# A transformer step on one core: when a lookup table is copied, and where 48 of 128 expert places run

## The reference

```
def peer_ffn(h, w_q, sub_k1, sub_k2, expert_u, expert_v):
...
    idx = jnp.take_along_axis(cidx, pos, axis=-1)
    gate = jax.nn.softmax(best, axis=-1).astype(h.dtype)
...
        u = jnp.take(expert_u, ib, axis=0)
        act = jax.nn.gelu(jnp.einsum('td,tkd->tk', hb, u))
        vrows = jnp.take(expert_v, ib, axis=0)
        return jnp.einsum('tk,tkd->td', gb * act, vrows)
```

## Time and profile before

| | us |
|---|---|
| median of 3 runs | 4420.11 (4410.85 to 4426.94) |
| the profiled execution's own time | 4409.17 |
| its span in the trace | 4407.6 |

### The profile page before, as it was taken

The page is one execution under the profiler, slowest core; times in us unless marked ns, Lnnn a source line. Parts: engine busy times, 40 slices in busy tenths (PEclk is TensorE's granted clock), DMA queues, the critical chain, the costliest instruction groups (busy, mean ns, idle before and its releaser), DMA issues.

```text
span 4407.6 us, 32479 instructions
## 1 busy us (share of the span) xinstructions
PE 3313.6 (75%) x8957; PEld 1651.8 (37%) x8957; DVE 2481.5 (56%) x4999; ACT 1047.2 (24%) x2847; POOL 1860.9 (42%) x1668
## 2 busy tenths in 40 slices
PE   8666289899926767634987887887887887777776
PEld 5443156556624434312433332333332332222222
DVE  0122055987338777744575675675675675675544
ACT  2101011011112211110333333333333332332322
POOL 0032025776125455510445445445445445445554
PEclk9876599999957877767999999999999999999999
DMA  5698987999388888851999999999999999999998
GB/s 217 218 334 315 320 270 303 395 386 369 140 345 329 298 314 336 295 195 73 370 414 421 420 418 421 404 417 421 407 418 422 404 419 422 418 411 421 422 419 356
DMA packets 301854, 1552.96 MB, mean 352 GB/s; under 512 B 31217, under 2 KB 58865, under 8 KB 179185
## 3 DMA queue, kind: packets, MB, share of 16 engines
q0 software_dynamic: 239616, 1342.28, 77.0%
q1 hardware_dynamic: 47488, 187.83, 11.0%
q10 hardware_dynamic: 14592, 21.10, 1.3%
HBM read 1507.98 MB, written 178.52 MB: 383 GB/s over the span
## 4 chain that ended last, share of the span: by engine, by line
DMA 25%; PE 16%; issue 6%; DVE 3%; ACT 1%; POOL 1%; ACTq 0%; POOLq 0%; DVEq 0%
DMA ring<-uv_d,IXD_p 25%; PE ps L1460 14%; PE ps L1430 3%; DVE ring L1661 2%; POOL ring L1778 1%; ACT dg L1510 1%; ACT GE_p L1504 0%; DVE BV_p L926 0%; DVE ACC L1642 0%; DVE DOT_p L1661 0%; DVE BP_p L931 0%; ACTq L1509 0%; PE ps L1445 0%; PE ps L1423 0%; POOLq L1774 0%
## 5 line engine op out<-in xcount | busy, mean ns | idle before, releaser
L1460 PE MATMUL ps<-ring,dg 128*128 128x512 f32 x3584 | 1699.7, 611 | 455.2 <-ACT dg L1510 432.7
L1778 POOL DMA_INDIRECT ring<-uv_d,IXD_p x896 | 1120.2, 1250 | 1308.3 <-PE ps L1460 1011.4
L1661 DVE CUSTOM_DVE_ANT_0 ring<-ring,H 128x1024 f32<-128x1024 f32 x896 | 1094.6, 1224 | 878.2 <-DMA ring<-uv_d,IXD_p 862.8
L1460 PEld LDWEIGHTS ps<-ring,dg 128*128 128x128 f32 x3584 | 651.5, 192 | 1381.7 <-ACT dg L1510 711.0
L1137 PE MATMUL ps<-w,xg 128*128 128x368 f32 x1792 | 563.6, 476 | 22.4 <-issue 20.2
L1504 ACT ACTIVATE GE_p<-DOT_p 128x2 f32<-128x2 f32 x448 | 91.1, 203 | 1473.3 <-DVE DOT_p L1661 1473.3
L1137 PEld LDWEIGHTS ps<-w,xg 128*128 128x128 f32 x1792 | 342.7, 191 | 242.9 <-issue 30.8
L1510 ACT ACTIVATE dg<-gdi,GE_p 128x128 f32<-128x128 f32 x896 | 310.7, 394 | 55.0 <-PE ps L1460 7.2
L1498 ACT ACTIVATE gdi<-ident,GD_p 128x128 f32<-128x128 f32 x896 | 303.3, 386 | 14.8 <-issue 14.6
L225 POOL DMA_DIRECT2D uv_d<-in_peer_u x128 | 69.4, 543 | 495.1 <-issue 253.9
L1260 POOL DMA_INDIRECT rv<-in_peer_v,IXD x128 | 156.9, 1226 | 260.2 <-DVE AC L1242 229.9
(11 more groups left out here) (364 smaller groups left out, 2718.0 us busy)
## 6 DMA issues: line engine op xcount, KB each, us to landing
uv_d<-in_peer_u POOLq DMA_DIRECT2D x128, 512.0 KB
uv_d<-in_peer_v POOLq DMA_DIRECT2D x128, 512.0 KB
w<-in_w_in SPq DMA_DIRECT2D x8, 2944.0 KB
w<-in_w_in SPq DMA_DIRECT2D x16, 1472.0 KB
z_d<-zo ACTq DMA_DIRECT2D x16, 1288.0 KB
ring<-uv_d,IXD_p POOLq DMA_INDIRECT x896
gates_p<-z_d SPq DMA_DIRECT2D x7, 1536.0 KB
wq_s<-in_peer_w_q SPq DMA_DIRECT2D x8, 1024.0 KB, 13.2
```

The lines of the kernel that those rows point to most:

```text
L1460: mm = T.matmul(bank(6 + n), dg[:, k % DR, :], ring[:, k % RS, D + n * 512:D + (n + 1) * 512], start=(k == 0), stop=(k == NK - 1))
L1661: V.tensor_tensor_reduce(out=row, in0=row, in1=H2[:], scale=1.0, scalar=0.0, op0=ALU.mult, op1=ALU.add, accum_out=DOT[:, k:k + 1]).then_in ...
L1778: g.indirect_dma_start(ring[:, n % RS, :], None, uv_d, bass.IndirectOffsetOnAxis(ap=IXD[:, n:n + 1], axis=0)).then_inc(s_ring[n % RS], 16)
```

## The change

The table's copy leaves the sample stage, the stage of block 1 and the start of the projection stage (`TABLE_BS`, `TABLE_E` and `TABLE_S` are 0). Parts 0 to 15 are issued at the end of the projection stage, behind all its gathers; parts 16 to 127 in the mixer stage, four after each point. POOL now issues a part only when the part two before it has landed.

The first 48 places of block 1 run in the projection stage, behind the places of block 0, through the same ring (`dve_experts_ahead`); their sum goes through `ac_d` in DRAM to the mixer stage. The mixer stage has 80 places of block 1 left, four points in a block instead of six or seven. Point 0, which stood between the transposes and the scores, now stands behind the softmax next to point 1; after it come one point between the merge and the copy of `oaT`, and one before the residual. Of the values three groups are left behind the last block instead of seven. ACT's places move: `GATES_AT` 12 to 4, gelu of group g to `n` = 9 + 10g, and two more gelus at `n` = 92 and 100 and a third after 111.

```
-TABLE_BS, TABLE_E, TABLE_CS = 32, 62, 86
+TABLE_BS, TABLE_E, TABLE_S, TABLE_CS = 0, 0, 0, 16
+AHEAD = 48
...
-            with g.Fori(lo, hi) as part:
-                g.dma_start(uv_d[bass.ds(part * P, P), 0:D], rows(t["peer_u"], part)).then_inc(s_uv, 16)
-                g.dma_start(uv_d[bass.ds(part * P, P), D:], rows(t["peer_v"], part)).then_inc(s_uv, 16)
+            for part in range(lo, hi):
+                if part >= 2:
+                    g.wait_ge(s_uv[part % 2], 32 * (part // 2))
+                    g.sem_inc(s_pool, 1)
+                g.dma_start(uv_d[part * P:(part + 1) * P, 0:D], rows(t["peer_u"], part)).then_inc(s_uv[part % 2], 16)
+                g.dma_start(uv_d[part * P:(part + 1) * P, D:], rows(t["peer_v"], part)).then_inc(s_uv[part % 2], 16)
...
-            dve_point(v, blk, 0)
             v.wait_ge(s["scores"], blk + 1)
...
             dve_probs(v, blk, 2 * P)
+            dve_point(v, blk, 0)
             dve_point(v, blk, 1)
-            dve_point(v, blk, 2)
             if merge:
                 dve_merge(v, blk - 1)
...
-            dve_point(v, blk, 3)
+            dve_point(v, blk, 2)
...
-            dve_point(v, blk, 4)
-            dve_point(v, blk, 5)
-            if blk == NB - 1:
-                dve_point(v, blk, 6)
+            dve_point(v, blk, 3)
...
-                    V.tensor_copy(IXD1[:], IX[:])
+                    V.tensor_copy(IXD1[:], IX[:]).then_inc(d["ixd"], 1)
...
+        def dve_experts_ahead(v):
...
+            for n in range(2 * AHEAD):
+                kind, grp = ORDER1[n // UG]
...
+                if kind == "u":
+                    V.tensor_tensor_reduce(out=row, in0=row, in1=H2A, scale=1.0, scalar=0.0, op0=ALU.mult,
+                                           op1=ALU.add, accum_out=DOT[:, k:k + 1]).then_inc(d["freed"], 1)
...
+                    V.scalar_tensor_tensor(ACCA, row, WG[:, k:k + 1], ACCA, ALU.mult, ALU.add).then_inc(d["freed"], 1)
...
-            GATES_AT, GATES1_AT = 12, 70
+            GATES_AT, GATES1_AT = 4, 56
...
-                return (n - 16) // 12 if 16 <= n < 16 + 12 * PH and (n - 16) % 12 == 0 else None
+                return (n - 9) // 10 if 9 <= n < 9 + 10 * PH and (n - 9) % 10 == 0 else None
...
+                    sp.wait_ge(d["freed"], RING + 2 * NK + 2 * AHEAD)
+                    sp.dma_start(ac_d, ACCA).then_inc(s_ac, 16)
...
-                    pool_table(g, TABLE_E, TABLE_CS)
+                    pool_table(g, TABLE_E, TABLE_S)
...
-                    pool_gathers(g, 0)
-
-        PG = 3
-        SET = 6 * PG
-        SETS = NK // SET
+                    pool_gathers(g, 0, ORDER, IXD)
+                    pool_gathers(g, 1, ORDER1, IXD1)
+                    pool_table(g, TABLE_S, TABLE_CS)
+
+        PG, PTS = 3, 4
+        SET = PTS * PG
+        SETS = (NK - AHEAD) // SET + 1
+        REST = NK - AHEAD
...
-                            if TABLE_CS + grp < NEXP // P:
-                                pool_table(g, TABLE_CS + grp, TABLE_CS + grp + 1)
-                    for grp in range(LAST - 6, LAST + 1):
+                            pool_table(g, TABLE_CS + 4 * grp, TABLE_CS + 4 * grp + 4)
+                    for grp in range(LAST, TAIL):
                         pool_values(g, grp)
```

More of the change, by code:

```diff
@@ L114, in trunk_kernel @@
         uv_d = dram("uv_d", (NEXP, 2 * D))
+        ac_d = dram("ac_d", (P, D))
         ps = ctx.enter_context(nc.psum_tensor("ps", [P, 8, 512], f32))
@@ L900, in act_norm, with pool_gathers @@
             S.activation(m4[:, 2:3], m4[:, 1:2], ACT.Sqrt).then_inc(d["sq"], 1)
-        def pool_gathers(g, blk):
+        def pool_gathers(g, blk, order, index):
             g.wait_ge(d["ixd"], blk + 1)
             g.sem_inc(d["pool"], 1)
-            for n in range(2 * NK):
-                kind, grp = ORDER[n // UG]
+            for n in range(len(order) * UG):
+                kind, grp = order[n // UG]
                 if n % 4 == 0:
@@ L1071, in dve_experts @@
             V.scalar_tensor_tensor(X1[:], ACC[:, 0], m4[:, 3:4], nf[:], ALU.mult, ALU.mult).then_inc(d["yo"], 1)
+        def dve_experts_ahead(v):
+            v.wait_ge(s_h2, 32)
+            v.wait_ge(d["gtc"], 3)
+            base = 2 * NK + RING
+            for n in range(2 * AHEAD):
+                kind, grp = ORDER1[n // UG]
+                k = grp * UG + n % UG
+                if kind == "v" and n % UG == 0:
+                    cols = slice(grp * UG, (grp + 1) * UG)
+                    v.wait_ge(d["gelu"], PH + grp + 1)
+                    V.tensor_tensor(WG[:, cols], GE[:, cols], GD1[:, cols], ALU.mult).then_inc(d["wgt"], 1)
+                    v.wait_ge(d["wgt"], PH + grp + 1)
+                row = ring[:, n % RING, :]
+                v.wait_ge(s_ring[n % RING], USES * 16 + 16 * (n // RING + 1))
+                if kind == "u":
+                    V.tensor_tensor_reduce(out=row, in0=row, in1=H2A, scale=1.0, scalar=0.0, op0=ALU.mult,
+                                           op1=ALU.add, accum_out=DOT[:, k:k + 1]).then_inc(d["freed"], 1)
+                    if n % UG == UG - 1:
+                        v.wait_ge(d["freed"], base + n + 1)
+                        v.sem_inc(d["act"], 1)
+                elif k == 0:
+                    V.tensor_scalar(ACCA, row, WG[:, k:k + 1], None, ALU.mult).then_inc(d["freed"], 1)
+                else:
+                    v.wait_ge(d["freed"], base + n)
+                    V.scalar_tensor_tensor(ACCA, row, WG[:, k:k + 1], ACCA, ALU.mult, ALU.add).then_inc(d["freed"], 1)
         with ExitStack() as m:
@@ L1085, in trunk_kernel @@
             SC1 = sb(m, "SC1_s", [P, 16, NKEY])
+            H2A, ACCA = [SC1[:, 8 * i:8 * i + 8, :].rearrange("p k n -> p (k n)") for i in range(2)]
             PB = NB - 2
@@ L1279, in _ @@
                     sp.dma_start(H21[:], rows(h2_d, 1)).then_inc(s_h2, 16)
+                    sp.dma_start(AC1[:], ac_d).then_inc(s_ac, 16)
                     load_gates(sp, 2)
```

84 lines of the change are left out of this document (48 added, 36 removed).

## The result

| | before | after |
|---|---|---|
| median (nine runs each) | 4420.11 us (4410.85 to 4435.35) | 4441.98 us (4433.79 to 4469.41) |
| profiled execution | 4409.17 us, span 4407.6 | 4441.98 us, span 4440.2 |

The ratio is 1.0056, with a 95% interval of 1.003 to 1.0083: slower, by 22 us, where 68 were forecast. Between the two profiled executions it is 33 us, against the same 68.

What follows compares the result with a forecast made beforehand. The prediction took the DMA engines as the bound and their idle time in the four stages before the last as deciding. Its terms, -14 - 42 + 78 + 46 = +68 us on 4420, gave 4488 us, range 4400 to 4555.

Steps and rivals of the forecast that it cites:

- The sample stage's -14: Sample stage: without the copy `wo_s` lands some 14 us earlier and the chain behind it moves along; bounds 0 and -19.
- block 1's -42: Block 1's stage: its end, a barrier, waits for POOL's transfers; without parts it ends 42 us earlier; bounds -7 and -45.
- +78: Projection stage: earlier first gather, 96 more gathers and 16 parts at its end make it 78 us longer; bounds +60, +95.
- 1.67 each: Projection stage: 256 gathers took 428 us, at the DMA's pace; 96 more at this price cost 160 us.
- the mixer term: Mixer stage: +46 us, from six blocks +41, first block +15 and tail -10; bounds -34 and +130.
- My low bound, 3.15: Mixer stage: a copy at 3.15 us per part, with gathers at 1.25, gives 91 us per block and a term of -34.
- six blocks, +41: Mixer stage: a block takes 102 us instead of 95, which over six blocks adds 41 us.
- The check by idle time: Four stages ahead of the last: DMA engines idle 336 us after against 269 before, +67 us.
- Faster: Rival, mixer stage: parts fill gaps at 3.15 us, gathers keep 1.25, a block takes 91 us; 4390 us, chance 0.17.
- Pacing: Rival, 128 parts: waits for landings leave the DMA engines empty, 80 us more; 4568 us, chance 0.15.
- Another cause of the gap: Rival, block 1's end: the gap at 471 to 517 us keeps 35 us; 4478 to 4523 us, chance 0.07.
- No change: Rival, whole kernel: large terms of both signs sum to +3 us; 4423 us, chance 0.11.

Runs made afterwards that it cites:

- gap_ten: The kernel before with ten of the 30 parts of block 1's stage issued at the start of the projection stage instead; 4335.14 us, one run.
- before_again: The kernel before, unaltered, run once more beside the follow-up kernels for its stage lengths there; 4379.24 us.
- mix_free: The changed kernel with no pacing of the parts in the mixer stage; 4407.67 us, ratio 1.0062 to the kernel before.
- mix_none: The changed kernel with the mixer stage's 112 parts all issued behind its last gathers, still paced; 4672.82 us.

## Why the prediction was right or wrong

**Direction and stages.** Slower, as given at 0.72, and inside the range of 4400 to 4555. The sample stage's -14 (wo_s now takes 13.3 us to land, half of the earlier trace rows), block 1's -42, and the barrier behind it came out; gap_ten shows the mechanism by itself. In the projection stage the first gather at +141.6 (138 forecast), the end 9 us behind the last part and the cost of the 16 parts (54 for 55) came out. Its sum, +80 for +78, is luck. The 352 gathers took 565 us from first to last issue, where 581 stood, and from the last gather to the stage's end it took 77 us, where 55 + 8 stood. The "1.67 each" came from a profile in which PE's pauses held up the evictions and with them the gelus: before_again has 397 us for 256 gathers, 1.55 each. And +78 was held against a stage that the same pauses had made 29.6 us longer; without them it is +91.6.

**The step that failed** is the mixer term, +46 where +7.6 was measured, and in it the DMA engines' work per block: "16 parts x 3.5 = 56 us, 24 gathers x 1.36 = 33 us, and the loads of queue 1 [...]: 99 us", and "With few bubbles I take 102". Queue 0 takes 82.7 us per block in the profile after (84.0% of four blocks of 98.5) instead of 89. At the gather's price without copy that is 1.56 us for a gather, more than I took, and 2.8 for a part instead of 3.5. With 11 us on queue 1 it is 94, and the period there is 98.5, not 102. The 3.5 was the time per part of a stretch that the copy fills nearly alone, in which the engines spent 3.3; it was carried over to a stage in which gathers run beside it. My low bound, 3.15, came from the copy with little beside it and was still too high. The second mistake of the same term is its count of blocks: it took all six as alike, as the next paragraph shows.

**Where the 38 us went.** By blocks: the start of the stage to the first merged store, two blocks, took 202.6 instead of 189.4 us, +13.2 where 15 and one block's 7 stood, 9 less. The next four periods took +17.9 together, 4.5 each instead of 7, 10 less. The fifth, block 8, took 93.1 instead of 103.3, -10.2 where +7 stood, 17 less: the kernel before had a seventh point in it, which the text of the change said and my sum of "six blocks, +41" did not use. In before's trace that point's two dots take DVE from 1877.2 to 1885.8 us, of which it waits 6.2:

```profile
1882.32 1.23 DVE L1225 CUSTOM_DVE_ANT_0 ru<-ru,H 128x1024 f32<-128x1024 f32 x1 [5.14 <-DMA ru<-in_peer_u,IXD]
```

The changed kernel has only 8 of its usual 12 dots left for block 8. The tail gave -13.4 instead of -10. So of the 38 us 10 lie in the four middle periods, 17 in block 8, 9 in the first two blocks and 3 in the tail.

**The check by idle time** was right in its sum and wrong in its use. By the windows, 96, 71, 102 and 68 us idle are 337, the forecast 336. But busy time was not constant: it fell from 1525 to 1488 us for 1.6 MB more. The fall is all on queue 0, whose 402.70 MB took 62.7% of 1794 us before and 59.5% of 1826 after, 1125 and 1086 us; queue 1 took 341 and 340. That the parts which left the first two stages for the mixer stage's mix are its cause rests on the price of a part above and is argued, since the gathers' price may differ between stages too. The fall, and not the idle time, is why +33 stands in the place of +67.

**The rivals.** Faster: half of its mechanism, parts that cost less in the mix, is what happened; its gathers at 1.25 us are not (1.56), and the period was 97 to 98, not 91. Pacing: 2 us per block by mix_free, 13 us in the mixer stage where 80 were taken, and the intervals of the two ratios overlap by a little. Another cause of the gap: excluded by gap_ten. No change: the result lies 9 us above its 0.3%.

**What I did not see** is that the change was two. Its half with the places shortens the chain of a block, by 14 us of DVE and 12 gathers, and was worth 76 us; I priced it only by the DMA, since I took the DMA engines to be the bound before as well. before_again's period of 94.2 at a share of 0.87 was a mixed bound, and so is 97.9 at 0.96.

## What to carry to other kernels

Price a transfer in the company it will have: a rate taken from a stretch in which a copy runs alone does not hold beside gathers. Where a change bundles two moves, sum them apart, each against the period that the other leaves. Filler transfers belong where the DMA engines idle and must land before the next thing that waits, be it a barrier, a weight load or a first gather: here that took the kernel with the places moved from 39 us slower than before, by the medians, to 94 us faster, with the same 128 parts.

## What the runs showed of the hardware

- A copy from DRAM to DRAM takes 3.46 us of the 16 DMA engines per 1.05 MB alone and paced (mix_none), 3.2 to 3.3 unpaced beside a stage's loads (before), and adds 2.45 (six per 24 gathers) to 2.9 us (twenty) beside row gathers, if a gather keeps its 1.56 us. At sixteen it is 2.8 with pacing and without.
- The end of a stage waits for POOL's transfers to land, 3.5 us for each part still in the queue (gap_ten against before_again), though in the kernel before no instruction of the program waits for them until the last stage.
- The same kernel ran 0.9% apart in two comparisons (4420 and 4381 us). Of the 30 us between the two profiles all lie in the projection stage (704.6 against 675.0), where PE starts matmuls 1.4 to 3.5 us apart in some stretches, at a granted clock of 0.59 in the one from 775 to 797 us; the last stage differs by 0.6 us.
